# One product of 512 columns for the high and low token halves of gate, query and key

## The reference, cut to what matters

```
xn = rms_norm(x, norm_mix_g)
z = xn @ w_in
rnn_x, rnn_gate, q, k, v, g_rnn, g_attn = split(z)
xc = causal_depthwise_conv(rnn_x, conv_w, conv_b)
hr = rg_lru(xc, ...)
y_rnn = (hr * gelu(rnn_gate)) @ w_proj_rnn
q = partial_rotary(q);  k = partial_rotary(k)
y_attn = attention(q, k, v) @ w_proj_attn
x = x + (sigmoid(g_rnn) * y_rnn + sigmoid(g_attn) * y_attn) @ w_out
x = x + moe_ffn(rms_norm(x, norm_ffn_g), ...)
return rms_norm(x, norm_final_g)
```

## Time and profile before

| | |
|---|---|
| median of the runs | 1171.51 us |
| the profiled execution, its own time | 1172.5 us |
| its span (first to last instruction) | 1170.8 us |
| mean granted TensorE clock | 0.986 of full speed |
| PE busy | 1104.9 us (94%), 7579 products |
| DVE busy | 361.3 us (31%) |
| ACT busy | 236.7 us (20%) |
| transfers | 449.17 MB, mean 384 GB/s |
| L545, 256 products | 64.3 us busy, 288 ns each |
| L546, 256 products | 63.1 us busy, 283 ns each |

### The profile page before, as it was taken

One profiled execution on the slowest core, in us unless ns is written; L12 is line 12 of the kernel. 1 busy time (PEld: TensorE's weight loads), 2 busy tenths in 40 slices (PEclk: granted clock), 3 DMA queues, 4 the chain that ended last, 5 costly groups with the idle time before them and its releaser, 6 DMA issues.

```text
span 1170.8 us, 17324 instructions
## 1 busy us (share of the span) xinstructions
PE 1104.9 (94%) x7579; PEld 559.4 (48%) x7579; DVE 361.3 (31%) x677; ACT 236.7 (20%) x435; POOL 7.9 (1%) x22
## 2 busy tenths in 40 slices
PE   8999999999999999999998989898989889898997
PEld 8999888884333333333333333333333333333332
DVE  7747975555121112211111111111111111111112
ACT  6678566343000000000000000000000000000002
POOL 0000000001000000000000000000000000000000
PEclk9999999999999999999999999999999999999999
DMA  9655557699999999999999999999999999999995
GB/s 275 256 188 181 198 216 269 242 405 399 428 427 432 429 430 429 429 433 429 432 431 430 434 433 433 430 431 432 432 430 431 434 432 431 433 431 431 430 424 224
DMA packets 46125, 449.17 MB, mean 384 GB/s; under 512 B 6145, under 2 KB 9281, under 8 KB 29890
## 3 DMA queue, kind: packets, MB, share of 16 engines
q1 hardware_dynamic: 45664, 447.70, 91.8%
q10 hardware_dynamic: 418, 0.84, 0.4%
HBM read 446.96 MB, written 1.05 MB: 383 GB/s over the span
## 4 chain that ended last, share of the span: by engine, by line
PE 56%; DMA 37%; DVE 4%; ACT 2%; issue 1%; SPq 0%; ACTq 0%; DVEq 0%
DMA dn_whole<-in_w_down 34%; PE ps L910 14%; PE ps L851 12%; PE ps L900 6%; PE ps L566 6%; PE ps L572 3%; PE ps L828 2%; PE ps L545 2%; PE ps L549 2%; PE ps L546 2%; DMA dn<-in_w_down 2%; PE ps L756 1%; PE ps L779 1%; PE ps L819 1%; DMA land<-in_w_in 1%
## 5 line engine op out<-in xcount | busy, mean ns | idle before, releaser
L851 PE MATMUL ps<-gu,xg 128*64 128x512 f32 x1920 | 418.7, 594 | 1.3 <-DMA gu<-in_w_gu 1.3
L851 PEld LDWEIGHTS ps<-gu,xg 128*64 128x64 f32 x1920 | 135.0, 137 | 271.7 <-issue 264.0
L910 PE MATMUL ps<-dn_whole,actT 128*64 128x512 f32 x672 | 161.9, 638 | 33.4 <-DMA dn_whole<-in_w_down 33.4
L1757 DVE TENSOR_SCALAR g<-ps 128x512 f32<-128x512 f32 x32 | 22.1, 692 | 441.2 <-PE ps L851 433.8
L910 PEld LDWEIGHTS ps<-dn_whole,actT 128*64 128x64 f32 x672 | 49.6, 146 | 144.6 <-issue 95.2
L1332 ACT ACTIVATE act_s<-g 128x512 f32<-128x512 f32 x25 | 15.7, 630 | 443.0 <-DVE g L1757 443.0
L1715 DVE TENSOR_TENSOR xg<-ps,vec 128x512 f32<-128x512 f32 x31 | 21.4, 690 | 178.9 <-PE ps L779 178.9
L1307 ACT ACTIVATE y_hi<-ps,stat 128x512 fp32r<-128x512 f32 x31 | 21.3, 687 | 250.2 <-PE ps L910 168.1
L900 PE MATMUL ps<-dn,actT 128*64 128x512 f32 x320 | 70.9, 594 | 0.6 <-DMA dn<-in_w_down 0.4
L545 PE MATMUL ps<-x_hi,w_hi 128*128 128x256 f32 x256 | 64.3, 288 | 1.1 <-DVE x_lo L1425 1.1
L546 PE MATMUL ps<-x_lo,w_hi 128*128 128x256 f32 x256 | 63.1, 283 | 0.0
(11 more groups left out here) (269 smaller groups left out, 1019.1 us busy)
## 6 DMA issues: line engine op xcount, KB each, us to landing
gu<-in_w_gu SPq DMA_DIRECT2D x52, 4096.0 KB, 30.8
dn_whole<-in_w_down SPq DMA_DIRECT2D x21, 4096.0 KB, 20.7
dn<-in_w_down SPq DMA_DIRECT2D x20, 2048.0 KB, 13.9
gu<-in_w_gu SPq DMA_DIRECT2D x18, 2048.0 KB, 13.4
land<-in_w_in SPq DMA_DIRECT2D x13, 2048.0 KB, 8.0
gu<-in_w_gu SPq DMA_DIRECT2D x12, 1024.0 KB, 8.4
land<-in_w_proj_rnn SPq DMA_DIRECT2D x2, 2048.0 KB, 7.8
land<-in_w_proj_attn SPq DMA_DIRECT2D x2, 2048.0 KB, 8.9
```

Of the source, the lines that this page charges most:

```text
L851: last = mm(ps[64 * h:64 * h + 64, 4 + c, :], xg[:, k * SLOTS:(k + 1) * SLOTS], gu[par][m // 2][:, m % 2 * 2 + r, c * D + h * HALF:c * D + ...
L910: last = mm(ps[64 * h:64 * h + 64, bank, :], actT[:, j // 2, j % 2 * SLOTS:(j % 2 + 1) * SLOTS], dn_whole[:, j, h * HALF:(h + 1) * HALF], ...
```

## The change

The tokens are laid in one tile `x_both`, high ones first and low ones behind, so that `x_hi` and `x_lo` are its two halves. Groups 4 to 15 (gate, query, key) no longer call `transposed` but `both_at_once`: for each piece eight products of 512 columns take high and low tokens together and leave the two results in the two halves of one bank, and the eight products with the low weight add into the second half. A group now fills two banks, one for each piece, and the groups take turns between banks 0, 1 and banks 2, 3. ACT's eviction copies the first halves; DVE then adds the second halves (`add_rest`) and counts `summed`. That add stands in `split_both(h)` behind the two splits of group h and is for group h-2. PE's groups from 6 on, up to 18, and both `swap_rope` wait for `summed` where they waited for `evicted`. Groups 0 to 3 keep the old form, in banks 0 to 3. The four empty counts of `evicted` at ACT's start are gone, and the other thresholds are renumbered for that.

```diff
+PAIRED = 4
-        x_hi, x_lo = at("x_hi", 112, [P, KT, T], f32r), at("x_lo", 168, [P, KT, T], f32r)
+        x_both = at("x_both", 112, [P, 2, KT, T], f32r)
+        x_hi, x_lo = x_both[:, 0], x_both[:, 1]
...
+            def both_at_once(h):
+
+                for c in range(2):
+                    b = (2 * h + c) % PIECES
+                    bank = h % 2 * 2 + c
+                    pe.wait_ge(hi_ready, 2 * h + c + 1)
+                    for k in range(KT):
+                        mm(ps[:, bank, :], w_hi[:, b, k, :], x_both[:, :, k, :], start=k == 0, stop=False)
+                    pe.wait_ge(lo_ready, 2 * h + c + 1)
+                    for k in range(KT):
+                        last = mm(ps[:, bank, T:2 * T], w_lo[:, b, k, :], x_hi[:, k, :], start=False, stop=k == KT - 1)
+                last.then_inc(filled, 1)
...
             for h in range(16):
-                pe.wait_ge(evicted, h + 1)
-                transposed(h, h % 4, x_hi, x_lo, first=h == 0)
+                if h < PAIRED:
+                    transposed(h, h, x_hi, x_lo, first=h == 0)
+                else:
+                    if h < PAIRED + 2:
+                        pe.wait_ge(evicted, 2 * (h - PAIRED) + 2)
+                    else:
+                        pe.wait_ge(summed, h - PAIRED - 1)
+                    both_at_once(h)
...
                 if h % 2 == 0:
-                    pe.wait_ge(evicted, h + 2)
+                    pe.wait_ge(summed, h // 2 + 3)
                 by_rows_of(h, h // 2 % 2 * 2, x_hi, x_lo)
...
-                    A(z[:, 2 * (h % 4):2 * (h % 4) + 2, :], ps[:, h % 4, :].rearrange("p (c t) -> p c t", c=2),
-                      ACT.Copy).then_inc(evicted, 1)
+                    b = h % 2 * 2
+                    y = ps[:, h, :].rearrange("p (c t) -> p c t", c=2) if h < PAIRED else ps[:, b:b + 2, 0:T]
+                    A(z[:, 2 * (h % 4):2 * (h % 4) + 2, :], y, ACT.Copy).then_inc(evicted, 1)
...
             def swap_rope(i, z):
 
-                act.wait_ge(evicted, 4 + 12 + 4 * i)
+                act.wait_ge(summed, 8 + 4 * i)
...
+            def add_rest(h):
+
+                dve.wait_ge(evicted, h + 1)
+                z = (z_gate, z_q, z_k)[h // 4 - 1][:, 2 * (h % 4):2 * (h % 4) + 2, :]
+                b = h % 2 * 2
+                V.tensor_tensor(z, z, ps[:, b:b + 2, T:2 * T], ALU.add).then_inc(summed, 1)
+
             def split_both(h):
 
                 split_lo(2 * h)
                 split_lo(2 * h + 1)
+                if PAIRED + 2 <= h < 18:
+                    add_rest(h - 2)
```

More of the change, by code:

```diff
@@ L216, in program @@
         hi_ready, lo_ready, filled, evicted = sem("hi_ready"), sem("lo_ready"), sem("filled"), sem("evicted")
+        summed = sem("summed")
         gu_landed = [[sem(f"gu_landed{p}_{m}") for m in range(2)] for p in range(2)]
@@ L646, in times_v @@
                 if i == 0:
-                    pe.wait_ge(evicted, 4 + 20)
+                    pe.wait_ge(evicted, 20)
                 if i >= 1:
@@ L666, in _ @@
                 if h % 2 == 0:
-                    pe.wait_ge(evicted, h + 2)
+                    pe.wait_ge(evicted, h - 2)
                 by_rows_of(h, h // 2 % 2 * 2, x_hi, x_lo)
@@ L1099, in _ @@
             act.dma_start(vec[:, :, :], vecs.rearrange("p (n k) -> p n k", n=N_VEC)).then_inc(vec_landed, 16)
-            for _ in range(4):
-                act.nop().then_inc(evicted, 1)
             act.wait_ge(spare_ready, 1)
@@ L1202, in _ @@
             swap_rope(1, z_k)
-            act.wait_ge(evicted, 4 + 8)
+            act.wait_ge(summed, 4)
             A(z_gate[:, :, :], z_gate[:, :, :], ACT.Gelu_apprx_tanh).then_inc(gelu_ready, 1)
@@ L1238, in _ @@
                     exps(i)
-            act.wait_ge(evicted, 4 + 28)
+            act.wait_ge(evicted, 28)
             A(z_gr[:, :, :], z_gr[:, :, :], ACT.Sigmoid).then_inc(zsig_ready, 1)
@@ L1446, in conv @@
                 if j % 2 == 0:
-                    dve.wait_ge(evicted, 4 + j // 2 + 1)
+                    dve.wait_ge(evicted, j // 2 + 1)
                     if j == 0:
```

## The result

The changed kernel takes 1181.52 us (median of 4 runs, 1179.95 to 1184.79) against 1171.42 us (4 runs, 1171.29 to 1171.87): a ratio of 1.0088, 95% interval 1.0075 to 1.0101. It is slower by 10.1 us where the prediction said 5.8, and outside the predicted range. The profiled execution took 1179.95 us, the shortest of the four; its span is 1178.2 us.

A forecast was written before the change was run, and what follows sets the result against it. PE was taken to bound the mixer, meeting DVE at the first score, and transfers the experts. A later score (4.3 us) plus the lower clock (1.5 us) on 1171.5 us gave 1177.3 us, range 1174.5 to 1180.0.

The forecast's parts named there:

- Four adds in a full stretch: DVE from about 94 us to the first score: no gap takes the adds, so the score comes 4.3 us later.
- PE's saving: PE in groups 4 to 15: a piece takes 2.78 us instead of 2.88; twelve groups save 2.4 us.
- The add: DVE's add of second halves: 0.60 us of DVE each, 0.68 us until its count; bounds 0.55 and 0.9 us.
- The first stall: PE ahead of group 6 waits 1.7 us for group 4's add behind DVE's splits; group 6 starts 1.35 us later.
- The query's transfer: On ACT: waits for the add of group 11, so issued at 90.5 us, 1.5 us later than before.
- The stalls of PE: PE ahead of groups 14, 15 and 16 waits for adds: 1.5, 0.9 and 3.05 us.
- The clock: At the start of group 16: PE's wait brings the lower clock level, costing 1.5 us (between 0 and 1.7).
- The shift stays to the end: Behind the first score: every microsecond by which the mixer ends later reaches the program's end, one for one.
- Rival 4: DVE between 94 and 126 us is not on the path; PE's saving comes through: 1169.1 us; chance 0.04.
- Rival 1: The clock stays up after the wait ahead of group 16: 1175.8 us; chance 0.25.
- Rival 2: Behind the score the shift is partly taken up, by 2 us or more: 1173.3 us; chance 0.08.
- Rival 3: 512 columns bring nothing (0.24 us) or adds cost 0.9 us: 1178.5 us each, 1179.7 both; chance 0.13.

The follow-up runs named there:

- experiment 1: Changed kernel, but SP issues the weight block of groups 20 and 21 only when the key's transfer has landed: 1177.05 us, ratio 1.0033.
- experiment 2: Changed kernel with 13 products on constants, results unused, filling PE's wait ahead of group 16: 1182.44 us, ratio 1.0084.
- experiment 3: Changed kernel with the block held until the key's transfer has landed and PE's wait ahead of group 16 filled: 1176.72 us, ratio 1.0043.
- experiment 4: Kernel before, with one value-neutral DVE operation behind the splits of group 17, for which the key's transfer waits: 1178.88 us, ratio 1.0054.
- experiment 5: Changed kernel without DVE's twelve adds, waits back on `evicted`, second halves left out of the result: 1171.19 us, ratio 0.9994.
- experiment 6: Changed kernel with the new form only for groups 4 to 10, the old form for 11 to 15: 1172.06 us, ratio 1.0004.
- experiment 7: As experiment 3, but each product of 512 columns is two of 256 with the same weight: 1177.43 us, ratio 1.0047.
- experiment 8: Changed kernel, but SP holds the block of groups 20 and 21 only until ACT has issued the key's transfer: 1177.15 us, ratio 1.0047.
- experiment 9: As experiment 3, but blocks of groups 16, 17 and 20, 21 wait only for issue of the query's and key's transfers: 1176.17 us, ratio 1.0035.

## Why the prediction was wrong

The first four columns are of one profiled execution each, the last of the medians of one set of runs. "Rotation" is the first step of the key's rotation on DVE (116.62 us before).

| kernel | key's transfer, to landing | rotation later by | score later by | `dn` issue later by | time later by |
|---|---|---|---|---|---|
| changed | 7.5 us | 9.4 | 9.4 | 9.4 | 10.1 |
| 1, block after landing | 3.3 | 4.7 | 6.3 | 6.2 | 4.3 |
| 2, wait filled | 7.7 | 10.1 | 10.8 | 10.7 | 9.7 |
| 3, both | 3.3 | 4.8 | 4.8 | 4.8 | 4.0 |
| 4, old kernel, late transfer | 7.6 | 6.6 | 8.3 | 8.2 | 6.1 |
| 5, no adds | 3.3 | -0.9 | -0.9 | -0.9 | -0.8 |
| 6, groups 4 to 10 | 3.3 | -0.2 | -0.2 | -0.1 | 0.1 |
| 7, pairs of 256 | 3.3 | 5.5 | 5.5 | 5.5 | 5.5 |
| 8, order only | 3.3 | 4.8 | 6.1 | 6.0 | 5.2 |
| 9, both transfers ahead | 3.3 | 3.9 | 3.9 | 4.0 | 3.9 |

The rotation and the score tell the two mechanisms apart. In seven kernels (before, changed, 3, 5, 6, 7 and 9) the score starts 9.44 us behind the rotation: DVE's steps set it. In experiments 1, 2, 4 and 8 it starts 1.6, 0.7, 1.7 and 1.3 us later than that, and in each of them PE had lost time at the lower clock behind its last wait ahead of the score, so that PE set it. So the 9.4 us of the changed kernel are all the late rotation: 4.4 us from the later issue of the key's transfer (116.93 against 112.52) and 5.0 us from the transfer itself. Its clock took nothing there.

**The step that failed** is in "Four adds in a full stretch": "DVE waits 1.9 us where it waited 0.96. The rotation moves from 116.62 to 120.95". It moved the issue of the key's transfer from 112.52 to 116.85 us (measured 116.93) and kept 4.1 us from issue to rotation. It took 9.1. The prediction said itself that DVE's splits of group 17 end at 116.1 us, and these release SP's next block; SP's queue was never laid beside ACT's. The reorder of the two issues could have been worked out from the profile of before. Its price, 5 us, could not: the transfer was never behind a block there. Experiments 1, 8 and 4 show it from three sides: undone by a later block, undone by the order of issue alone, and made in the old kernel.

In the changed kernel the second half of the transfer landed at 125.9 us (issued at 117.5, 8.4 us), the block at 127.2 (116.32, 10.9 us in the view of the transfers). The same view by window, from 116 to 121 us and from 121 to 127 us:

```profile
q1 hardware_dynamic: 533, 1.09, 67.5%
```

```profile
q1 hardware_dynamic: 507, 1.01, 76.1%
q10 hardware_dynamic: 64, 0.26, 18.3%
```

Not one packet of the small transfer runs before 121 us, 4.2 us behind its issue, when half of the block is through; from there on both queues' packets run side by side. In all nine cases of a small transfer issued behind a block (listed in the last section) its first packet comes 4.2 to 4.4 us behind its issue, after 548 to 578 of the block's packets; before the change the key's came 1.2 us behind its issue.

The Trainium skill ("DMA: Bandwidth & Descriptors", section "Queues, rings and completion order") says that a transfer engine takes turns between the queues that have work, packet by packet. Read plainly, and with the packets of the view taken for the page's, four packets on each of 16 engines for the small transfer (64 in all) beside some 65 for the block would be through early. From 121 us on the trace agrees, in that both queues run; for the 4.2 us before it the rule does not account. What held the small packets in that time is open: no run here looked inside the queues.

**PE's saving** held: a piece takes 2.79 us (from one L565 to the next, 92.94 to 95.73; 2.78 predicted), the two runs of 256 cost nothing, and L562 follows at 0.23 us (1.84 us for eight), the pace of the earlier trace rows. The Trainium skill's rule ("TensorE: Matmul & The Clock Gate", section "Wait — 56ns, not 53.3ns?"), the columns at 2.4 GHz plus some 2.5 ns for each product, does not hold here, as the prediction had read from its rows: an estimate from that page's figure gives a loss of 0.04 us a group in experiment 7; a group lost 0.18.

**The add** held: 0.67 to 0.68 us each, from two banks as from one.

**The first stall** was mis-sized: 1.7 us predicted, 0.31 in the changed kernel, none in experiment 3, and 0.76 to 1.20 in the six others that keep this add. It hangs on when DVE gets to the splits of group 6 (46.17 us in the earlier trace rows, 45.06 in the changed kernel), and that on when an earlier weight block lands: ACT stood 2.80 us for it before and 1.5 in the changed kernel. A term that stands on one execution's load times should have had a range of a microsecond. ACT's splits of group 13 came 0.74 us sooner for it (85.77 against 86.51), and the query's transfer gave that back at DVE. That experiment 3 came within 0.5 us of the 4.3 worked out is in part luck: a stall that did not come and a wait that was left out go opposite ways.

**The query's transfer** was issued at 89.85 us (90.5 predicted). What the prediction left out is that it, too, fell behind a block, and that DVE would wait for it.

**The stalls of PE** were 1.31, 1.33 and 2.73 us (1.5, 0.9 and 3.05 predicted), and the last ended at 113.93 us against 113.8.

**The clock** fell where it was said to. Its price at the score is the difference of experiments 1 and 3, 1.5 us, the predicted value; experiment 8 against 3 gives 1.3. The agreement in size owes something to luck: the lower level lasted 6.8 us in the changed kernel and 3.4 in experiments 1 and 8, and the prediction had one size for both. In the changed kernel the fall lasted longer and cost PE 2.9 us (the 24 products of group 16 take 8.47 us, from 113.93 to 122.40, and 5.57 us, from 114.29 to 119.86, in experiment 2), but there PE had cover behind the late rotation, so the sum of the two mechanisms is not their sum in time. A late rotation also makes a fall of its own: PE stands 4.20 us in experiment 2 and 5.64 in experiment 4 behind it, and the clock is down afterwards.

**The shift stays to the end**: right for the mixer, where every row of the table has the same shift at `dn` as at the score. From there to the end the difference of the medians is between 2.2 us below that shift (experiment 4) and 0.7 us above it (the changed kernel), and no experiment was made on this part. One for one holds to about 2 us and is not shown more finely: in experiment 1 the interval of the ratio (2.2 to 5.6 us) does not reach the 6.2 us at `dn`. The changed kernel's four runs spread over 4.8 us, the old kernel's over 0.6 in the same set, but over 3.4 in another; whether the change spreads them is open. Of the 10.1 us, 9.4 are shown by place in one execution; the rest is within that spread.

**The rivals.** Rival 4 was refuted at the place that it named: the key's transfer did wait for the last add. Rival 1's world (clock up, and the transfer as quick as before) is experiment 3, 4.8 us at the score against 4.3. Rival 2 is not settled below 2 us, by the paragraph above; its own time was worked out wrongly, too: 2 us absorbed gives 1175.3 us, and 1173.3 needs 4. Rival 3 is refuted by the pace (1.84 us for eight) and the add (0.67 to 0.68 us); an add of 0.9 would have cost 0.22 us more each, not 0.3, and the page's pace 1.0 us in six groups, not 1.1. None of the four named the queue.

No version beats the kernel before. With PE's saving and every repair the adds still cost 4 us (experiment 9), and with no adds at all (experiment 5) the gain is 0.8 us, which the interval (0.9985 to 1.0003) does not tell from nothing.

## What to carry to other kernels

When an edit moves the issue of a small transfer that an engine waits for, list what every other queue issues within a few microseconds of it, by what releases each, and see whether the order of the two flips; here 1.6 us of relative delay were worth 5. A saving on a busy engine is worth nothing until the engines that meet it at the next common point save time too: PE's 2.2 us (twelve groups of 0.18) gave 0.9 at best, and the work handed to DVE lay on the path in full. And where two mechanisms overlap, undo each alone and both together, and read the granted clock up to the mark that counts in every run: filling one wait only moved the fall to the next, and 1.5 us came back once the transfer was mended as well.

## What the runs showed of the hardware

- A transfer of 2 x 128 KB issued 0.6 to 0.7 us behind one of 2 MB, on another engine's queue, landed after 7.4 to 7.7 us (median of the halves) in nine cases (the key's in the changed kernel and experiments 2 and 4, the query's in the changed kernel and experiments 1, 2, 3, 7 and 8). Its packets did not begin until 4.2 to 4.4 us behind the issue, when about half of the 2 MB was through. Issued 1.0 to 1.4 us ahead of the 2 MB it landed after 3.3 us, the same as with no block near. There was one exception: the query's in experiment 6, 1.0 us ahead, took 3.2 to 4.5 us, and at the same distance the kernel before took 3.2 to 3.4.
- PE idle for 2.7 us was followed by the lower clock in all three kernels where that wait stood (the changed one, experiments 1 and 8), and PE idle for 4.20 and 5.64 us in experiments 2 and 4 too. The lower level lasted 6.8 us in the changed kernel and experiment 4 and 3.4 us in experiments 1, 2 and 8 (in windows of 0.25 us), and in experiment 1 it began 1.5 us after PE was at work again. The eight products behind the wait of 2.7 us took 3.78, 2.55 and 3.43 us, against 2.11 with the wait filled. What decides between the two lengths is open.
- A product whose 512 columns come as two runs of 256, 8 KB apart in a row of the tile, keeps the pace of a single run (0.23 us against 0.2275), and an add that reads 2 x 256 from two banks takes as long as one from a single bank (0.67 to 0.68 us against 0.68).
